# Eight-head mixer kernel: seven of the modulation units summed on GpSimd instead of VectorE

## The reference, cut to what matters

```python
c_act = jax.nn.silu(c)
mod = c_act @ w_ada[l] + b_ada[l]
sh1, sc1, g1, sh2, sc2, g2 = jnp.split(mod, N_MOD, axis=-1)
h = modulate(rms_norm(x, norm1_w[l]), sh1, sc1)
mix = hybrid_mixer(h, w_in[l], ...)
x = x + g1[:, None, :] * mix
```

## Time and profile before

| | |
|---|---|
| median of 3 runs | 1360.04 us (1358.09 to 1365.27) |
| the profiled execution's own time | 1357.97 us |
| its span, first to last instruction | 1356.3 us |
| PE busy | 1298.3 us (96%) |
| DVE busy | 946.3 us (70%) |
| ACT busy | 673.1 us (50%) |
| POOL busy | 15.6 us (1%), 84 instructions |
| the steps that hold the seven units | about 77 to 371 us of the span |

### The profile page before, as it was taken

One profiled execution on the slowest core, in us unless ns is written; L12 is line 12 of the kernel. 1 busy time (PEld: TensorE's weight loads), 2 busy tenths in 40 slices (PEclk: granted clock), 3 DMA queues, 4 the chain that ended last, 5 costly groups with the idle time before them and its releaser, 6 DMA issues.

```text
span 1356.3 us, 26717 instructions
## 1 busy us (share of the span) xinstructions
PE 1298.3 (96%) x9989; PEld 1218.3 (90%) x9989; DVE 946.3 (70%) x1686; ACT 673.1 (50%) x1171; POOL 15.6 (1%) x84
## 2 busy tenths in 40 slices
PE   6899999999999999999899988999999999999998
PEld 3899899998899999999678877999997887999997
DVE  0678888888867798878656644998886642786653
ACT  2555555555565655444555425554442443545543
POOL 4000000000000000000000000000000000000000
PEclk9899999999999999999899999999999999999999
DMA  9755546555354699879567552898796471976563
GB/s 328 206 173 171 162 119 202 171 171 169 116 183 140 175 282 276 254 236 321 164 219 251 184 155 78 248 279 268 216 320 203 153 211 33 292 211 180 149 198 95
DMA packets 400341, 270.01 MB, mean 199 GB/s; under 512 B 9978, under 2 KB 357488, under 8 KB 400256
## 3 DMA queue, kind: packets, MB, share of 16 engines
q1 hardware_dynamic: 400256, 268.83, 65.3%
HBM read 267.75 MB, written 1.05 MB: 198 GB/s over the span
## 4 chain that ended last, share of the span: by engine, by line
PE 84%; DVE 6%; ACT 3%; DMA 2%; issue 2%; SPq 2%; DVEq 0%; ACTq 0%
PE pair L808 21%; PE pair L809 21%; PE pair L810 21%; PE pair L885 3%; PE pair L1224 1%; PE pair L1015 1%; DVE w_low L1975 1%; PE bank L1023 1%; PE bank L770 1%; PE bank L1024 1%; ACT w_high L1424 1%; DMA ring<-in_mla_w_q_up 1%; SPq L552 1%; PE bank L750 1%; PE pair L1268 1%
## 5 line engine op out<-in xcount | busy, mean ns | idle before, releaser
L808 PE MATMUL pair<-x_space,w_high 128*128 128x258 f32 (+1 forms) x1888 | 557.1, 295 | 9.2 <-DVE x_space L2005 6.6
L809 PE MATMUL pair<-x_space,w_high 128*128 128x258 f32 (+1 forms) x1888 | 535.9, 284 | 0.0
L810 PE MATMUL pair<-x_space,w_low 128*128 128x258 f32 (+1 forms) x1888 | 532.2, 282 | 0.0
L1975 DVE TENSOR_TENSOR w_low<-w_raw,w_high 128x1024 fp32r<-128x1024 f32 (+2 forms) x348 | 390.3, 1127 | 95.7 <-ACT w_high L1424 88.9
L808 PEld LDWEIGHTS pair<-x_space,w_high 128*128 128x128 f32 x1888 | 358.5, 190 | 24.0 <-issue 15.4
L1424 ACT ACTIVATE w_high<-w_raw 128x1024 fp32r<-128x1024 f32 (+2 forms) x348 | 331.8, 978 | 81.9 <-DMA w_raw<-in_ffn_w_out 23.8
L809 PEld LDWEIGHTS pair<-x_space,w_high 128*128 128x128 f32 x1888 | 360.5, 191 | 1.3 <-issue 1.0
L810 PEld LDWEIGHTS pair<-x_space,w_low 128*128 128x128 f32 x1888 | 361.5, 191 | 0.0
L808 PE MATMUL pair<-act_parts,w_high 128*128 128x256 f32 x528 | 150.6, 285 | 0.0
L809 PE MATMUL pair<-act_parts,w_high 128*128 128x256 f32 x528 | 149.4, 283 | 0.0
L810 PE MATMUL pair<-act_parts,w_low 128*128 128x256 f32 x528 | 149.4, 283 | 0.0
(11 more groups left out here) (408 smaller groups left out, 1682.5 us busy)
## 6 DMA issues: line engine op xcount, KB each, us to landing
ada_w<-in_ada_w SPq DMA_DIRECT2D x48, 1024.0 KB, 6.0
w_raw<-in_ffn_w_in SPq DMA_DIRECT2D x88, 512.0 KB, 4.3
w_raw<-in_w_in SPq DMA_DIRECT2D x72, 512.0 KB, 3.7
w_raw<-in_w_ffn_in SPq DMA_DIRECT2D x44, 512.0 KB, 4.5
ada_w<-in_w_ada SPq DMA_DIRECT2D x16, 1024.0 KB, 7.2
w_raw<-in_gla_w_in SPq DMA_DIRECT2D x24, 512.0 KB, 6.3
w_raw<-in_ffn_w_out SPq DMA_DIRECT2D x32, 384.0 KB, 4.4
w_raw<-in_ffn_w_out SPq DMA_DIRECT2D x32, 320.0 KB, 3.5
```

The source lines that it names most:

```text
L808: pe.matmul(cols, hi[:, n, :], x_high[:, k, :], start=k == 0, stop=False)
L809: pe.matmul(cols, hi[:, n, :], x_low[:, k, :], start=False, stop=False)
L810: mm = pe.matmul(cols, lo[:, n, :], x_high[:, k, :], start=False, stop=k == kb - 1)
L1975: dve.tensor_tensor(w_low[:, s, 0:m], w_raw[:, s, 0:m], w_high[:, s, 0:m].bitcast(F32), ALU.subtract)\
```

## The change

The seven units of steps 1 to 7 leave DVE's list and go to the end of POOL's. A unit there is one multiply and then seven pairs, a multiply into `term` (the free slot of `w_raw`, first 512 columns) and an add to the accumulator. The factor, one number per partition, is read as a tensor broadcast over 512 columns. POOL waits for both halves of the weights before the first multiply, and for its own last instruction before each next one. It counts up `ada_used` after each half, as DVE did, and for the third unit on it waits until PE has read the accumulator. DVE's loop over pairs of heads becomes a loop over single heads. Everything else, SP's list, PE's and ACT's among it, is as it was.

```diff
+            term = w_raw[:, SplitStream.SLOTS - 1, 0:ADA]
+            for i in range(1, H1):
+                u, c = A_HEAD + i, i - 1
+                acc, mac = acc2[:, c % 2], MAC_HEAD + KB * c
+                if i >= 3:
+                    pool.wait_ge(S("ada_rows"), 1 + (i - 1) // 2)
+                for k in range(KB):
+                    w = ada_w[:, k // 4, k % 4, :]
+                    factor = cact[:, k, 31:32].broadcast_to([P, ADA])
+                    if k == 0:
+                        pool.wait_ge(S("ada_landed0"), 16 * u)
+                        pool.wait_ge(S("ada_landed1"), 16 * u)
+                    if k == 0:
+                        pool.tensor_tensor(acc, w, factor, ALU.mult).then_inc(S("ada_mac"), 1)
+                    else:
+                        pool.wait_ge(S("ada_mac"), mac + k)
+                        pool.tensor_tensor(term, w, factor, ALU.mult).then_inc(S("ada_term"), 1)
+                        pool.wait_ge(S("ada_term"), (KB - 1) * c + k)
+                        pool.tensor_tensor(acc, acc, term, ALU.add).then_inc(S("ada_mac"), 1)
+                    if k % 4 == 3:
+                        pool.wait_ge(S("ada_mac"), mac + k + 1)
+                        pool.sem_inc(S("ada_used"), 1)
...
-                def unit(*ks):
-                    if gemm:
-                        ada_unit(A_HEAD + i, 0, MAC_HEAD + KB * c, ks, acc=acc2[:, acc])
...
-                    if l >= LEVELS - 2:
-                        unit(l - LEVELS + 2)
...
                     if ch < NCH - 1:
-                        unit(2 + 2 * ch)
                         dve.wait_ge(S("s_done"), 3 * c + ch + 1)
...
-                        unit(3 + 2 * ch)
...
-            with dve.Fori(0, H1 // 2 - 1) as p:
-                head1(2 * p + 1, True)
-                head1(2 * p + 2, True, acc=1)
+            with dve.Fori(1, H1 - 1) as i:
+                head1(i, True)
```

More of the change, by code:

```diff
@@ L2125, in decay_rows, with head1 @@
                 dve.wait_ge(S("hcur"), c + 1)
-            def head1(i, gemm, last=False, acc=0):
+            def head1(i, gemm, last=False):
                 n = i
```

## The result

The changed kernel takes 1404.36 us (median of 4 runs, 1401.98 to 1408.84), the kernel before 1359.3 us (1358.09 to 1365.27): a ratio on record of 1.0315, 95% interval 1.0278 to 1.0352 (the two medians alone give 1.0332). It is 45 us slower; 1430 was forecast. Numbers of lines are now those of the changed kernel: `low` is L1998, the convolution L2096 (its first piece, one tensor) and L2099 (two tensors), the levels L2203, the chunks L2221 to L2230.

The account below looks back on a forecast made before the run. PE, busy 96% of the span, sets the pace. Contention less given-back wait, 10 us per step, 70 in all, on the 1356.3 us span gives 1426; against the 1360.04 median, 1430 us, range 1351 to 1455.

Parts of the forecast that it names:

- the case without contention: POOL's and DVE's SBUF instructions don't hold each other up; only given-back wait counts, 1352 to 1354 us; chance 0.23.
- What bounds the kernel, and what leaves DVE: Heads' stage: PE sets the pace; 5.7 us per step leaves DVE, but only PE's waits, 0.9 us per step, are gained.
- The gain that the sum had at 6.5 us: PE's waits for DVE's chunks and masks over seven steps, 5.9 to 7.9 us given back, taken as 6.5.
- the 0.9 us at the masks: PE's wait for the masks over seven steps, claimed to go since DVE comes to them earlier.
- The line through two sizes: POOL's adds, 214 ns at 16 columns and 455 at 128, extended to 1.28 us at 512 columns.
- POOL comes in time: A unit takes POOL some 20 us of the 34 available before SP would wait; PE's first accumulator read has 11 us margin.
- Taking turns: POOL and two-tensor DVE instructions each hold the SBUF path to their end: 10 us per step, 1400 to 1455; chance 0.62.
- the two bounds: DVE's loss to POOL's reading: nothing if they don't touch, up to 19.2 us per unit if instructions alternate.
- 11.8 us gross per step: PE's standstill in the heads' stage: last level 12.3 us late, less 0.54 us of slack; 10.9 net.
- the walk: One step priced instruction by instruction from POOL's start at 211 us: levels begin 0.7, 4.7, 8.5 and 12.3 us late.
- don't touch: Rival: POOL and DVE show no contention, only the given-back wait counts; 1353.5 us, between 1352 and 1354; chance 0.23.
- DVE keeps the path: Rival: DVE's next instruction always precedes POOL's; 0 to 3 us per step, 1355 to 1380, say 1368 us; chance 0.12.

## Why the prediction was right

The mechanism and the direction were right, the size less so: 1404 us is 26 below the forecast of 1430 and 45 above the kernel before, where 70 were forecast. That it lies in the range says little, for 1351 to 1455 takes in the case without contention as well.

**What bounds the kernel, and what leaves DVE.** Right in kind: 5.7 us less on DVE per step is worth under 1 us. The gain that the sum had at 6.5 us is 4.9 us by the runs, and 6.3 us at the end of the stage. Without arithmetic, from 70 to 440 us, PE's wait at the first chunk fell from 3.2 to 0.3 us and the one at the last from 4.3 to 2.3; the 0.9 us at the masks, which I had said would go, stayed (1.4 in that profile).

**What POOL gets.** The line through two sizes gave 1.28 us at 512 columns. The add takes 1.276 us at the shortest. The broadcast multiply, which I had priced the same, takes 1.04. Whether that comes from the broadcast operand or from multiplying instead of adding, no run separates: every instruction of this size with two full tensors was an add. POOL comes in time, as forecast: 229.69 to 252.23 us, 22.5 us for a unit.

**What POOL's reading does to DVE.** Taking turns was the right choice between the two bounds, and it is shown, not argued: the time falls by 47.7 us when only POOL's arithmetic goes, it follows the length of POOL's two-tensor instructions, and the rows show each engine standing still until the other's instruction ends. The Trainium skill ("SBUF — State Buffer", section "Who interferes with whom") says this of a DVE instruction with two SBUF inputs against a GpSimd instruction that reads SBUF, and of writing, that it touches only DVE's two-port modes. The trace agrees with both for two-tensor instructions and for memsets (478 ns untouched, 1004 instead of 348). It doesn't agree for POOL's one-tensor multiply, which also reads SBUF: 512 ns against 481, and a w_low that begins under it keeps its 1.21 us.

**The step that was off** is the size of this term: 11.8 us gross per step where the runs show about 6.8 (47.7 over seven). Two things in the walk were too dear.
- I put POOL's whole 1.28 us on top of DVE's whole 0.40 us for each convolution piece, 1.68 us. The rows give 3.48 us for three (239.57 to 243.05), 1.16 each. A piece ends 0.28 us after POOL's instruction, less than its own 0.40, so part of it overlaps the wait; and half of POOL's instructions are the shorter kind. A turn costs a short piece 0.76 us, not 1.28.
- I gave POOL a turn before every w_low. At 237.84 w_low was first, lost nothing, and POOL paid.

One slip went the other way: in the second and third level the walk leaves out L2184's own 0.61 us. Its prices add up to 8.06 us there, not 7.4, and would have made the last level 13.7 us late instead of 12.3. So the true error of the prices is larger than that of the sum.

The levels' spacing was 4.42, 6.06 and 6.00 us, where the walk had 7.5, 7.4 and 7.4. Counted from the w_low ahead of them (229.27 here, 211.20 before), the four full L2203 are 0.80, 1.71, 4.25 and 6.64 us late; the walk had 0.7, 4.7, 8.5 and 12.3. For the same reason w_low's mean rose to 1.39 us and not towards 2.4, and two unit loads lie 47.3 us apart and not 52. That the cost falls in three levels and stops with the fifteenth instruction was right. The rivals: "don't touch" and "DVE keeps the path" are out for this kernel; what comes nearest to the second is the one-tensor form, which it doesn't use.

## What to carry to other kernels

Work moved from DVE to POOL can still cost DVE time: two-tensor instructions on both engines take turns, so count what DVE loses per turn against the slack between two turns, not POOL's busy time against its idle time. If POOL must do arithmetic beside DVE, give it one-tensor forms (a number per partition instead of a broadcast tensor), though they are slower on POOL, and leave time between the rest; here even that only came near the kernel before (1.0032). Before giving work away, see what PE waits for: here most of the loss was that multiply-adds stood in front of one small instruction, and moving them within DVE's list won what the times say was to be won. And before moving work to a quieter place, look for the engine that reads its result.

## What was not expected of the hardware

- POOL's multiply by a number per partition takes 1.56 us for 128x512, half as long again as the same product with the factor as a broadcast tensor (1.04 us). It disturbs DVE ten times less (4 us against 40 us in the kernel's time).
- POOL's memsets, which read nothing, stretch DVE's one-tensor instructions threefold (348 to 1004 ns) and leave its two-tensor ones alone. It stood among the branches expected, but as part of the rival.
